# Two load buffers and six split buffers in a two-layer hybrid decoder kernel, with weight splits placed ahead of vector work and three projections on other PSUM banks

## The reference

```python
h = rms_norm(x, norm_g)
proj = jnp.einsum('bsd,de->bse', h, w_in)
...
y_a = mla_branch(q_lat, kv_lat, ...)
y_b = gated_deltanet_branch(dn_qkv, dn_a, dn_b, ...)
y_c = dilated_branch(dil_qkv, cos_h, sin_h, ...)
ys = jnp.stack([y_a * jax.nn.silu(z_a), y_b * jax.nn.silu(z_b), y_c * jax.nn.silu(z_c)], axis=2)
branch_out = jnp.einsum('bsnc,ncd->bsnd', ys, w_branch)
gates = jax.nn.sigmoid(gate_logits.reshape(B, S, N_BRANCHES, D_MODEL))
mixed = jnp.sum(gates * branch_out, axis=2)
return x + jnp.einsum('bsd,de->bse', mixed, w_out)
```

## Time and profile before

| what | value |
|---|---|
| time, median of 3 runs | 783.84 us (783.74 to 783.97) |
| profiled execution, its own time | 783.82 us |
| its span, first to last instruction | 782.0 us |
| PE, PEld, DVE, ACT, POOL busy | 97%, 84%, 75%, 61%, 22% |
| DMA | 124.97 MB, mean 160 GB/s, q1 50.7% of 16 engines |
| granted TensorE clock | 1.00 |

### The profile page before, as it was taken

One profiled execution on the slowest core, in us unless ns is written; L12 is line 12 of the kernel. 1 busy time (PEld: TensorE's weight loads), 2 busy tenths in 40 slices (PEclk: granted clock), 3 DMA queues, 4 the chain that ended last, 5 costly groups with the idle time before them and its releaser, 6 DMA issues.

```text
span 782.0 us, 12175 instructions
## 1 busy us (share of the span) xinstructions
PE 762.4 (97%) x4506; PEld 656.6 (84%) x4506; DVE 584.7 (75%) x846; ACT 476.6 (61%) x1073; POOL 175.2 (22%) x187
## 2 busy tenths in 40 slices
PE   7999999999999999999999999999999899999998
PEld 6999888878877888888899998888788778888886
DVE  6687878989887486776656886888997855958763
ACT  6869476678584654354457776765866576443451
POOL 1255105205031002411023511231222200116100
PEclk9999999999999999999999999999999999999999
DMA  8656544553645345455565563555345443555551
GB/s 244 209 191 200 160 143 131 155 164 108 196 156 162 105 138 189 135 188 173 150 197 181 162 192 106 177 159 165 113 156 164 136 158 96 182 185 160 171 182 54
DMA packets 73041, 124.97 MB, mean 160 GB/s; under 512 B 9757, under 2 KB 17047, under 8 KB 72983
## 3 DMA queue, kind: packets, MB, share of 16 engines
q1 hardware_dynamic: 72560, 124.13, 50.7%
q10 hardware_dynamic: 423, 0.06, 0.0%
HBM read 122.06 MB, written 1.05 MB: 157 GB/s over the span
## 4 chain that ended last, share of the span: by engine, by line
PE 81%; DVE 9%; ACT 7%; issue 2%; DMA 1%; SPq 0%; ACTq 0%; DVEq 0%
PE bank L787 20%; PE bank L789 20%; PE bank L788 20%; PE bank L769 3%; PE bank L771 3%; PE bank L770 3%; ACT w_hi L1130 2%; DVE w_lo L1464 2%; ACT at L1196 2%; PE bank L817 1%; ACT at L1399 1%; ACT at L1199 1%; DVE dn L1664 1%; DVE gate L1818 1%; PE bank L927 1%
## 5 line engine op out<-in xcount | busy, mean ns | idle before, releaser
L1464 DVE TENSOR_TENSOR w_lo<-raw,w_hi 128x1024 fp32r<-128x1024 f32 (+4 forms) x240 | 288.8, 1234 | 81.3 <-ACT w_hi L1130 78.5
L787 PE MATMUL bank<-w_hi,hT 128*128 128x512 f32 (+2 forms) x704 | 278.5, 396 | 11.8 <-DVE w_lo L1464 5.4
L1130 ACT ACTIVATE w_hi<-raw 128x1024 fp32r<-128x1024 f32 (+4 forms) x239 | 235.0, 1018 | 84.7 <-PE bank L789 73.3
L789 PE MATMUL bank<-w_hi,hT 128*128 128x512 f32 (+2 forms) x704 | 270.9, 385 | 0.0
L788 PE MATMUL bank<-w_lo,hT 128*128 128x512 f32 (+2 forms) x704 | 270.7, 385 | 0.0
L787 PEld LDWEIGHTS bank<-w_hi,hT 128*128 128x128 f32 x704 | 132.8, 189 | 41.9 <-DVE w_lo L1464 9.9
L789 PEld LDWEIGHTS bank<-w_hi,hT 128*128 128x128 f32 x704 | 132.7, 188 | 25.7
L788 PEld LDWEIGHTS bank<-w_lo,hT 128*128 128x128 f32 x704 | 133.0, 189 | 22.6
L1937 POOL TENSOR_TENSOR sm<-sm,tab 128x8 f32<-128x8 f32 (+3 forms) x46 | 62.7, 1362 | 218.8 <-ACT dn L1344 78.7
L769 PE MATMUL bank<-hT,w_hi 128*128 128x256 f32 x192 | 54.9, 286 | 0.0
L771 PE MATMUL bank<-hT,w_lo 128*128 128x256 f32 x192 | 54.3, 283 | 0.0
(11 more groups left out here) (228 smaller groups left out, 966.6 us busy)
## 6 DMA issues: line engine op xcount, KB each, us to landing
raw<-in_w_in SPq DMA_DIRECT2D x168, 512.0 KB, 4.3
raw<-in_w_branch SPq DMA_DIRECT2D x24, 512.0 KB, 4.4
raw<-in_w_out SPq DMA_DIRECT2D x16, 512.0 KB, 4.3
raw<-in_w_in SPq DMA_DIRECT2D x8, 384.0 KB, 5.5
raw<-in_w_in SPq DMA_DIRECT2D x8, 320.0 KB, 4.2
raw<-in_mla_w_kv_b SPq DMA_DIRECT2D x8, 256.0 KB, 2.9
raw<-in_mla_w_q_b SPq DMA_DIRECT2D x4, 384.0 KB, 3.5
xs<-in_x SPq DMA_DIRECT2D x2, 512.0 KB, 5.1
```

What stands on the lines that cost most here:

```text
L787: mm(o, src[0][:, a, tok], hi[:, k, :], start=starts and p == k == 0, stop=False)
L789: last = mm(o, src[1][:, a, tok], hi[:, k, :], start=False, stop=ends(u, p) and k == k1 - k0 - 1)
L1130: av(view(w_hi, q % SPLIT, k1 - k0, n), view(raw, q % RAW, k1 - k0, n), ACT.Copy).then_inc(hi_done, 1)
L1464: tt(view(w_lo, q % SPLIT, k1 - k0, n), view(raw, q % RAW, k1 - k0, n), view(w_hi, q % SPLIT, k1 - k0, n).bitcast(F32), ALU.subtract).then ...
```

## The change

Five edits. `RAW` goes from 4 to 2 and `SPLIT` from 5 to 6; the three buffers keep 56 KB per partition together (4+5+5 slots of 4 KB before, 2+6+6 after). By the larger `SPLIT`, each split stands one piece further ahead in `ORDER`, and one more split stands at the start. The mark `("ahead",)` is put before `d_rs`, `d_rope` and `dn_S` in units 20 to 36, so that the second split of these units comes before that work. The substitution is spread over 10 units in place of 8, and what follows it moves back and is packed closer. The projections `dil` 3, 5 and 7 go to banks 2 and 3.

```diff
-SOLVE_FIRST, SOLVE_UNITS = 27, 8
+SOLVE_FIRST, SOLVE_UNITS = 27, 10
...
-RAW, SPLIT = 4, 5
+RAW, SPLIT = 2, 6
...
-    put(36, ("dn_X",))
-    put(37, ("dn_kd",), ("dn_TX",))
-    put(38, ("dn_u", 0), ("dn_u", 1), ("dn_w",))
-    put(40, ("dn_ds", 0))
-    put(41, ("dn_ws", 1), ("dn_dec", 1))
...
-    put(46, ("dn_oc", 0), ("dn_oc", 1), ("dn_o", 0), ("dn_o", 1))
-    put(47, ("dn_oss", 0), ("dn_oss", 1), ("dn_on",))
+    put(38, ("dn_X",))
+    put(39, ("dn_kd",), ("dn_TX",))
+    put(40, ("dn_u", 0), ("dn_u", 1), ("dn_w",))
+    put(41, ("dn_ds", 0))
+    put(42, ("dn_ws", 1), ("dn_dec", 1))
...
+    put(47, ("dn_oc", 0), ("dn_oc", 1), ("dn_o", 0), ("dn_o", 1))
+    put(48, ("dn_oss", 0), ("dn_oss", 1), ("dn_on",))
     for g in range(GROUPS):
         b = 20 + 6 * g
-        put(b, ("d_rs", g, 0), ("d_rope", g, 0), *([("d_scale", g, 0)] if g in APART else []))
-        put(b + 2, ("tr", "dq", 2 * g), ("tr", "dq", 2 * g + 1), ("d_rs", g, 1), ("d_rope", g, 1),
+        put(b, ("ahead",), ("d_rs", g, 0), ("d_rope", g, 0), *([("d_scale", g, 0)] if g in APART else []))
+        put(b + 2, ("tr", "dq", 2 * g), ("tr", "dq", 2 * g + 1), ("ahead",), ("d_rs", g, 1), ("d_rope", g, 1),
...
     for n in range(SOLVE_UNITS):
-        put(SOLVE_FIRST + n, ("dn_S", n))
+        put(SOLVE_FIRST + n, ("ahead",), ("dn_S", n))
...
-             (0, ("xT", 2)), (0, ("xT", 3)), (0, ("norm",))]
+             (0, ("xT", 2)), (0, ("xT", 3)), (0, ("norm",)), (0, ("prep", 2, 0))]
...
-    return t + {("latq", 0): 2, ("qb", 0): 2, ("dn", 1): 2, ("kvb", 1): 4, ("dn", 2): 2}.get(UNITS[u][:2], 0)
+    return t + {("latq", 0): 2, ("qb", 0): 2, ("dn", 1): 2, ("kvb", 1): 4, ("dn", 2): 2, ("dil", 3): 2, ("dil", 5): 2, ("dil", 7): 2}.get(UNITS[u][:2], 0)
```

More of the change, by code:

```diff
@@ L151, in step_table @@
     put(24, ("ahead",), ("dn_kkE",), ("dn_Uc",), ("dn_qkE",), ("dn_G",))
-    put(36, ("dn_X",))
-    put(37, ("dn_kd",), ("dn_TX",))
-    put(38, ("dn_u", 0), ("dn_u", 1), ("dn_w",))
-    put(40, ("dn_ds", 0))
-    put(41, ("dn_ws", 1), ("dn_dec", 1))
[L157 to L160, removed]
-    put(46, ("dn_oc", 0), ("dn_oc", 1), ("dn_o", 0), ("dn_o", 1))
-    put(47, ("dn_oss", 0), ("dn_oss", 1), ("dn_on",))
+    put(38, ("dn_X",))
[3 more added lines that the diff above has]
+    put(42, ("dn_ws", 1), ("dn_dec", 1))
+    put(43, ("dn_ds", 1))
+    put(44, ("dn_ws", 2), ("dn_dec", 2))
+    put(45, ("dn_ds", 2))
+    put(46, ("dn_ws", 3))
+    put(47, ("dn_oc", 0), ("dn_oc", 1), ("dn_o", 0), ("dn_o", 1))
+    put(48, ("dn_oss", 0), ("dn_oss", 1), ("dn_on",))
     for g in range(GROUPS):
         b = 20 + 6 * g
-        put(b, ("d_rs", g, 0), ("d_rope", g, 0), *([("d_scale", g, 0)] if g in APART else []))
-        put(b + 2, ("tr", "dq", 2 * g), ("tr", "dq", 2 * g + 1), ("d_rs", g, 1), ("d_rope", g, 1),
+        put(b, ("ahead",), ("d_rs", g, 0), ("d_rope", g, 0), *([("d_scale", g, 0)] if g in APART else []))
+        put(b + 2, ("tr", "dq", 2 * g), ("tr", "dq", 2 * g + 1), ("ahead",), ("d_rs", g, 1), ("d_rope", g, 1),
             ("d_scale", g, 1), *([("dn_row",), ("dn_kk",), ("dn_qk",)] if g == 0 else []))
```

## The result

The changed kernel takes 924.55 us (median of 4 runs, 921.4 to 925.39) against 783.9 us, a ratio of 1.179 with a 95% interval of 1.178 to 1.180: 141 us slower. Forecast were 819 us and a range to 860 us. The direction and the name of the mechanism were right; the loss was four times the one forecast.

A forecast was written before the change was run, and what follows sets the result against it. PE's matmuls, busy 97% of the span, were taken to set the length. Span 782.0 + 40 (two load buffers) + 5 (start-up) - 10 (placing) = 817 us, with 1.8 us around it 819 us; range 787 to 860 us.

The forecast's parts named there:

- What two load buffers cost: Loop of load, ACT half, DVE half against demand per pair, by stretch: +6 to +91 us, taken as +40.
- sparse stretches: 84 to 165 and 165 to 278 us, repeated in layer two: pairs wanted every 7.4 and 7.5 us, no excess.
- from bunching: Part of the +40 us: 2 us put down for the stretches other than start, dense ones and second layer's start.
- high bound: Slot loop with today's waits inside a split kept: 3.4 us landing plus 3.6 us split, 7.0 us per pair.
- The dense stretches: First stretch, late in each layer, and second layer's start: loop exceeds demand, some 9, 10, 10 and 9 us.
- Start-up: First pieces wait for slots and SP's gain loads no longer overlap: +5 us, between 3 and 6.
- The worked chain: At the start: piece 5 goes out at 15.7 us, ready near 21.8 us, where PE started it at 19.49 us.
- The placing: Marks and banks remove PE's waits for DVE splits and ACT evictions: 8 to 12 us gained, 10 taken.
- The third rival: DVE work ahead of the second split is what PE awaits anyway; 10 us missing, 829 us; within the forecast's 0.64.
- The second rival: In-order queues of ACT, DVE and SP lock together, sparse stretches too: loop +60 to +91, 837 to 873 us; chance 0.20.
- The first rival: Two slots are enough: loop costs 0 to 8 us, placing's gain of 10 remains, 776 to 784 us; chance 0.16.
- the sign: Mostly in dense stretches: PE waits for w_lo and L1199 of 30 to 50 us in sum would show the forecast.

The follow-up runs named there:

- place_only: The changed kernel with four load and five split buffers as before, keeping marks, ten-unit substitution and banks, without the extra split at the start: 782.86 us, ratio 0.9986.
- marks_sub: The kernel before with dil 3, 5 and 7 on banks 2 and 3 and the mark put before dn_S alone: 784.74 us, ratio 1.0010.
- two_matmuls: The changed kernel without one of the three matmuls per weight block, so the product is less exact: 908.75 us, ratio 1.160.
- banks_only: The kernel before with projections dil 3, 5 and 7 on banks 2 and 3 and nothing else: 785.6 us, ratio 1.0015.

## Why the prediction was wrong

**The step that failed** is the sum over the stretches in "What two load buffers cost": "84 to 165 us ... No excess by either bound", "165 to 278 us ... None either". It compared the mean demand per pair (7.4 and 7.5 us) with a loop of 5.7 to 7.0 us. By the starts of DVE's halves the four sparse stretches of the two layers lost 9.3, 25.6, 9.4 and 25.3 us, 70 us in sum, where 2 us "from bunching" was put down. The sum lets the loop run beside the stretch's other work. With two slots it runs through that work: the load waits for a DVE half that stands behind the substitution, which stands behind the rotary step, which stands behind an eviction that stands behind the split of the piece loaded last. The loops measured in these stretches were 8.3 and 9.0 us, over the high bound of 7.0. The bound's 3.6 us inside a split were not too few: from the start of ACT's half to the end of DVE's they were 3.0 and 3.5 us. What it lacked was a term for the landed piece that waits for ACT, put at nothing and measured at 1.4 and 1.5 us, and the landing took 3.8 to 3.9 us for 3.4. Its own sentence "ACT and DVE take their steps in turn, so while ACT waits for a landing, the eviction behind it waits" has the mechanism, and the sum does not.

**The dense stretches** were named rightly and sized too low: 13.4, 13.4, 20.5 and 11.2 us (59.9 to 73.3, 107.1 to 120.5, 81.8 to 102.3, 106.0 to 117.2) in place of 9, 10, 9 and 10. A pair took 6.1 to 6.7 us there, inside 5.7 to 7.0. The end of the program, behind the last split, added 2.8 us, so that start-up, dense and sparse stretches and end make 10.6 + 58.5 + 69.6 + 2.8 = 141.5 us, the whole difference of the spans (141.3).

**Start-up**: the ninth piece's DVE half starts at 33.05 us for 22.48, 10.6 us later; forecast 5. The worked chain had piece 5 ready near 21.8 us (its own terms, 15.7 + 3.4 + 2.1, give 21.2). Its load went out at 15.86 us, as forecast, but took 6.35 us to land where 3.4 was put (it had taken 6.9 us in the kernel before, among the other transfers of the start). Its split is the second of these two:

```profile
21.70 0.98 DVE L1464 TENSOR_TENSOR w_lo<-raw,w_hi 128x784 fp32r<-128x784 f32 x1 [4.58 <-ACT w_hi L1130]
23.12 0.98 DVE L1464 TENSOR_TENSOR w_lo<-raw,w_hi 128x784 fp32r<-128x784 f32 x1 [0.45 <-ACT w_hi L1130]
```

It was ready at 24.1 us, and the following pairs, which the sum did not carry on, added the rest.

**The placing**: forecast -10 us, measured -1.1 us. The two waits went as said; that the next ones would take their place, and that one longer wait can bring the clock down, was not priced. The third rival had named the missing 10 us; its reason, that other DVE work is what PE waits for anyway, fits place_only in part (a wait for DVE at L1483 grew from 1.1 to 3.3 us) and not the clock in the other two runs.

**The second rival**, the queues locking together, was the nearest, at 0.20, with 837 to 873 us. Its price came from the same bound and was 50 us short: it speaks of the sparse stretches, but its +91 us hold nothing for them. Nothing in the forecast spoke of the clock.

**The first rival** (two slots are enough) fell. The Trainium skill advises in "Trainium Kernel Development and Optimization", Best Practices, to double-buffer so that DMA overlaps compute. In this case two slots did not give that overlap: with the same placing two cost 140 us over four, and three 22. A slot's mean loop does not tell how many are enough: 7.55 us against a piece wanted every 3.25 us asks for 2.3 slots, and three were still slower than four. The rival's range is also not the sum of its terms: 783.8 - 10 with 0 to 8 us for the loop is 774 to 782 us, not 776 to 784, and the start-up's 5 us are left out.

**What was right**: ACT's waits for the landing of `raw` in tens of us and more (308), DVE's waits behind them, and no `w_lo` wait left around the substitution. PE's waits for `w_lo` and for L1199 came to 36 us, inside the 30 to 50 named as the sign; but they are a third of its idle time, and the rest stands in other rows.

## What to carry to other kernels

A buffer's round trip is not the sum of its own steps: it passes through every queue in which one of them stands, so before taking a slot away, follow one trip in the trace and write down what stands ahead of each step, and what waits behind it, instead of comparing means over a stretch. A split that waits for its load in an in-order queue holds up the work behind it even when its own result is not wanted for long; here more result buffers did not help, and freeing the slot at an earlier engine did. And a wait removed from the engine that bounds is won only down to the next step that is nearly late. Count PE's idle time and its busy time apart when you look for the gain: in marks_sub one longer wait took the place of several short ones, and the slower clock behind it took back what they had cost.

## What the runs showed of the hardware

The granted clock of TensorE fell to half (the 1.2 GHz level) for 93 us in sum (mean 0.95), while its mean was 1.00 (2.4 GHz) in the kernel before. The first fall lies at the end of a wait of PE for ACT:

```profile
42.68 2.39 PE L847 MATMUL bank<-tab,at 128*128 128x128 f32 x10 [4.24 <-ACT at L1199]
```

Two stretches of 4 us behind it (busy time of the engines, then the clock as 0.50 and 1.00):

```profile
44.00:48.00 4.00, 4.00 (x21) 4.00 (x20) 2.26 (x7) 3.99 (x9) 0.32 (x1) 0.50 0.12 41
49.00:53.00 4.00, 4.00 (x35) 4.00 (x35) 1.87 (x4) 2.88 (x12) 2.07 (x4) 1.00 0.65 254
```

21 matmuls against 35 in the same time. PE was busy throughout both: the low clock came with the idle time and outlasted it. 93 us at half the clock can lengthen PE's work by up to 46 us, and its busy time grew by 41 us. In two_matmuls, where PE had more idle time, it was at half for 243 us, and the kernel was 16 us faster all the same: it costs where PE bounds, as in marks_sub and banks_only (3.6 and 2.8 us of busy time for 7 us at half), and in the changed kernel it mostly did not.
